# Gated linear attention by token, two heads at a time, in a two-layer encoder step

## What is computed

```python
    def step(S, inp):                       # one chunk, S is (64 x 128) a head
        qc, kc, vc, lac = inp
        cum = jnp.cumsum(lac, axis=1)
        last = cum[:, -1:]
        ref = 0.5 * last
        att = jnp.einsum('blhd,bshd->bhls', qc * jnp.exp(cum - ref), kc * jnp.exp(ref - cum))
        att = jnp.where(causal, att, 0.0)
        o = (jnp.einsum('bhls,bshe->blhe', att, vc)
             + jnp.einsum('blhd,bhde->blhe', qc * jnp.exp(cum), S))
        S = jnp.exp(last[:, 0])[..., None] * S + jnp.einsum('bshd,bshe->bhde', kc * jnp.exp(last - cum), vc)
        return S, o
...
    log_alpha = jax.nn.log_sigmoid(glr @ P['gla_w_gate'][j] + P['gla_b_gate'][j]) / GLA_TAU
    out_c = jax.nn.silu(gr) * _head_norm(o_c, P['gla_gn_g'][j])
```

## Times and profile before

| | |
|---|---|
| three runs | 1528.97, 1525.61, 1529.1 us, median 1528.97 |
| profiled execution | 1530.31 us, of which the span of its trace 1528.8 |
| busy | TensorE 1422.2 us, VectorE 714.6, ScalarE 494.3, GpSimd 85.0 |
| mean granted TensorE clock | 0.961 of full speed |
| items and decays of the GLA stage | about 773.9 to 947.2 us of the span |
| first mLSTM head | 947.2 to 967.7 us |

### The profile page before, as it was taken

One profiled execution on the slowest core, in us unless ns is written; L12 is line 12 of the kernel. 1 busy time (PEld: TensorE's weight loads), 2 busy tenths in 40 slices (PEclk: granted clock), 3 DMA queues, 4 the chain that ended last, 5 costly groups with the idle time before them and its releaser, 6 DMA issues.

```text
span 1528.8 us, 28545 instructions
## 1 busy us (share of the span) xinstructions
PE 1422.2 (93%) x11061; PEld 1346.7 (88%) x11061; DVE 714.6 (47%) x1243; ACT 494.3 (32%) x751; POOL 85.0 (6%) x101
## 2 busy tenths in 40 slices
PE   5999998989999999999879798998799999999997
PEld 3888887979999999999768686878799999999997
DVE  4664654564433333334663535774643333333344
ACT  4453354333222222222352324331332222222233
POOL 0000000001100110010000000000001001100100
PEclk9899999999999999999979798998899999999999
DMA  9444454665353335222212121331222232232222
GB/s 343 141 130 141 129 146 126 214 232 192 91 180 96 87 91 191 85 83 66 62 30 56 33 69 40 85 89 58 69 68 83 85 94 83 84 95 83 82 76 80
DMA packets 224520, 163.12 MB, mean 107 GB/s; under 512 B 9346, under 2 KB 209732, under 8 KB 224332
## 3 DMA queue, kind: packets, MB, share of 16 engines
q1 hardware_dynamic: 212864, 119.42, 26.8%
q10 hardware_dynamic: 6764, 25.30, 4.4%
q0 software_dynamic: 4832, 17.58, 3.6%
HBM read 158.68 MB, written 3.59 MB: 106 GB/s over the span
## 4 chain that ended last, share of the span: by engine, by line
PE 83%; DVE 6%; DMA 4%; ACT 3%; issue 3%; ACTq 1%; DVEq 0%; POOL 0%; POOLq 0%; SPq 0%
PE ring L555 71%; DMA mod_weight<-in_w_mod 2%; PE core_j L461 2%; DVE weight_low L423 1%; PE core_k L461 1%; DMA weight_raw<-in_a_w_out 1%; PE core_j L775 1%; ACT weight_high L418 1%; PE core_k L1159 1%; DMA mixer_area<-in_w_mod 1%; PE ring L1252 1%; PE core_k L1162 1%; ACTq L2050 1%; PE core_k L780 1%; DVE normed_low L653 0%
## 5 line engine op out<-in xcount | busy, mean ns | idle before, releaser
L555 PE MATMUL ring<-normed_high,weight_high 128*128 128x272 f32 x2128 | 453.6, 295 | 27.6 <-DVE normed_low L653 14.1
L555 PE MATMUL ring<-normed_high,weight_low 128*128 128x272 f32 x2128 | 446.3, 292 | 0.0
L555 PE MATMUL ring<-normed_low,weight_high 128*128 128x272 f32 x2128 | 445.9, 291 | 0.0
L555 PEld LDWEIGHTS ring<-normed_high,weight_high 128*128 128x128 f32 x2128 | 340.8, 192 | 36.9 <-issue 23.7
L555 PEld LDWEIGHTS ring<-normed_low,weight_high 128*128 128x128 f32 x2128 | 341.7, 193 | 0.0
L555 PEld LDWEIGHTS ring<-normed_high,weight_low 128*128 128x128 f32 x2128 | 339.0, 192 | 0.0
L423 DVE TENSOR_TENSOR weight_low<-weight_raw,weight_high 128x1024 fp32r<-128x1024 f32 x197 | 261.1, 1326 | 142.1 <-ACT weight_high L418 141.0
L418 ACT ACTIVATE weight_high<-weight_raw 128x1024 fp32r<-128x1024 f32 x197 | 207.0, 1051 | 180.0 <-PE ring L555 146.2
L555 PE MATMUL ring<-mixed_high,weight_high 128*128 128x272 f32 x960 | 203.9, 294 | 11.6 <-DVE weight_low L423 8.2
L555 PE MATMUL ring<-mixed_high,weight_low 128*128 128x272 f32 x960 | 201.5, 292 | 0.0
L555 PE MATMUL ring<-mixed_low,weight_high 128*128 128x272 f32 x960 | 200.9, 291 | 0.0
(11 more groups left out here) (370 smaller groups left out, 1026.0 us busy)
## 6 DMA issues: line engine op xcount, KB each, us to landing
weight_raw<-in_w_ffn_in SPq DMA_DIRECT2D x88, 512.0 KB, 4.0
mixer_area<-in_w_mod ACTq DMA_DIRECT2D x12, 2048.0 KB, 10.9
mod_weight<-in_w_mod POOLq DMA_DIRECT2D x16, 1024.0 KB, 5.9
weight_raw<-in_w_ffn_out SPq DMA_DIRECT2D x32, 512.0 KB, 4.1
weight_raw<-in_a_w_in SPq DMA_DIRECT2D x24, 512.0 KB, 5.7
weight_raw<-in_c_w_in SPq DMA_DIRECT2D x20, 512.0 KB, 4.2
mixer_area<-in_w_mod SPq DMA_DIRECT2D x7, 1024.0 KB, 13.6
weight_raw<-in_w_ffn_out SPq DMA_DIRECT2D x16, 384.0 KB, 3.4
```

Source lines behind the costliest of these rows:

```text
L555: last = pe.matmul(PS[p.slot][:, half, 0:HALF], w[n.slot][:, k, :], x[:, k, half * HALF:(half + 1) * HALF], start=(k == 0 and w is WH and ...
```

## The change

The GLA part is written anew.

- Decays: the two 16-row products write to `core_j` and `core_k`, between the two halves of the first item, and no longer through the ring. The gate rows of the mLSTM are turned later, before item 11.
- Scores: a head uses its own 64 rows of the key and query tiles as operands; the zeroed copies and their GpSimd memsets are gone.
- Key-value products: two products of 64 rows x 64 columns for each chunk, one a head, into the upper and lower half of one PSUM tile. One serial sum of states then serves both heads.
- Output: by token, the masked scores and queries as the stationary side, the values and states moving (128 columns).
- Norm: batch-norm statistics on ten blocks (five token blocks of two heads), one inverse root for both heads, the blocks normalised half by ScalarE and half by VectorE, then turned back by TensorE through the ring and multiplied by gain and gate.
- Order: items are value, key, query, value, gate, gate of pair 0, value, key, query, value of pair 1, u, gate, gate, o. SP's loads, waits and the tiles' places are changed to fit. In the first mLSTM head its q and k products stand ahead of its value product.

Cut to the parts that are spoken of:

```diff
+            for n, a in enumerate(GLA_COLS):
+                load_weight(sp, gla_w(n), CW, lambda: a)
+                if n == 1:
+                    sp.wait_ge(s_modp, FIRST_HALF + 12)
+                    gla_state(0)
+                if n == 8:
+                    sp.wait_ge(s_rexp, 2)
+                    for row, src in ((0, RA), (1, RI)):
+                        sp.dma_start(GATE_ROWS[row], src[0:HEADS, :]).then_inc(s_smw, 16)
+                if n == 9:
+                    gla_state(1)
+                if n == 10:
+                    ml_weights(0)
+                    sp.wait_ge(s_smw, 64)
+                    ml_decays(0)
+            sp.wait_ge(s_got, 2)
+            ml_states(0)
+            for h in range(1, HEADS):
+                load_weight(sp, ml_w(h, 0), CW, lambda: h * P + C_U)
+                load_weight(sp, ml_w(h, 1), CW, lambda: h * P + C_O)
+                ml_weights(h)
+                ml_decays(h)
+                ml_states(h)
             sp.wait_ge(s_rg, 1)
             sp.dma_start(out["m_p"][0].rearrange("a h -> h a"), RM[0:HEADS, TP - 1:TP],
...
+        def gla_kv_pe(pe, i):
+
+            pe.wait_ge(s_gvtok, 2 * i + 2)
+            pe.wait_ge(s_gatt, 2 * i + 2)
             for c in range(2 * NB):
                 r = slice(64 * (c % 2), 64 * (c % 2) + 64)
-                dst = (K, J)[c % 2][:, 0, (c // 2) * P:(c // 2 + 1) * P]
-                pe.matmul(dst, K4T[r, c // 2, :], VTG[r, c // 2, :], start=True, stop=True)
-            pe.matmul(K[:, 1, 0:P], K4T[0:TS, NB, :], VTG[0:TS, NB, :], start=True, stop=True).then_inc(s_gkv, 1)
-            fill()
-            pe.wait_ge(s_gst, n + 1)
+                for j in range(2):
+                    q = slice(64 * j, 64 * j + 64)
+                    pe.matmul((K, J)[c % 2][q, 0, (c // 2) * P:(c // 2 + 1) * P], K4T[r, c // 2, q],
+                              VTG[j][r, c // 2, :], start=True, stop=True)
+            for j in range(2):
+                q = slice(64 * j, 64 * j + 64)
+                mm = pe.matmul(K[q, 1, 0:P], K4T[0:TS, NB, q], VTG[j][0:TS, NB, :], start=True, stop=True)
...
+        def gla_out_pe(pe, i):
+
+            pe.wait_ge(s_gst, i + 1)
             pe.wait_ge(s_gs0, 16 * i + 16)
-            for c in range(2 * NB):
-                cols = slice(64 * c, 64 * c + 64)
-                pe.matmul(K[:, 0, cols], VTG[:, c // 2, :], AG[:, c // 2, 64 * (c % 2):64 * (c % 2) + 64],
-                          start=True, stop=(c == 0))
-                if c:
-                    pe.matmul(K[:, 0, cols], SG8[:, c - 1, :], Q3[j][:, cols], start=False, stop=True)
-            pe.matmul(K[:, 1, P:P + TS], VTG[0:TS, NB, :], AG[0:TS, NB, 0:TS], start=True, stop=False)
-            pe.matmul(K[:, 1, P:P + TS], SG0, Q3[j][:, TP:T], start=False, stop=True).then_inc(s_got, 1)
+            for j in range(2):
+                q = slice(64 * j, 64 * j + 64)
+                dst = (K, J)[j]
+                for b in range(NB):
+                    cols = slice(b * P, (b + 1) * P)
+                    if b:
+                        pe.matmul(dst[:, 0, cols], AG[j][:, b, :], VTG[j][:, b, :], start=True, stop=False)
+                    else:
+                        for r in (slice(0, 64), slice(64, P)):
+                            pe.matmul(dst[r, 0, cols], AG[j][:, b, r], VTG[j][:, b, :], start=True, stop=(r.start == 0))
+                    for c in (2 * b, 2 * b + 1):
+                        if c:
+                            pe.matmul(dst[64 * (c % 2):64 * (c % 2) + 64, 0, cols], Q3[q, 64 * c:64 * c + 64],
+                                      SG8[q, c - 1, :], start=False, stop=True)
+                pe.matmul(dst[0:TS, 1, 0:P], AG[j][0:TS, NB, 0:TS], VTG[j][0:TS, NB, :], start=True, stop=False)
+                mm = pe.matmul(dst[0:TS, 1, 0:P], Q3[q, TP:T], SG0[q], start=False, stop=True)
+            mm.then_inc(s_got, 1)
+
+        def gla_turn_pe(pe, i, j):
+
+            p = Turn(R_GLA + GLA_TURNED[i][j])
+            pe.wait_ge(*((s_on, i + 1) if j else (s_o, HEADS + i + 1)))
+            pe.wait_ge(s_free[p.slot], p.before)
+            for b in range(NB):
+                pe.transpose(PS[p.slot][:, 0, b * P:(b + 1) * P], ON2[:, j * (NB + 1) + b, :], IDENT)
+            pe.transpose(PS[p.slot][:, 1, 0:TS], ON2[0:TS, j * (NB + 1) + NB, :],
+                         IDENT[0:TS, 0:TS]).then_inc(s_otr, 1)
+
...
+            for n in (1, 2):
+                item(n)
+            gla_keys_pe(pe, 0)
+            gla_values_pe(pe, 0, 0)
+            item(3)
+            pe.wait_ge(s_k4tok, 1)
+            gla_scores_pe(pe, 0, 0)
+            pe.wait_ge(s_gvtok, 1)
+            gla_values_pe(pe, 0, 1)
+            item(4)
+            pe.wait_ge(s_gatt, 1)
+            gla_scores_pe(pe, 0, 1)
+            item(5)
+            gla_kv_pe(pe, 0)
+            item(6)
+            gla_out_pe(pe, 0)
+            for n in (7, 8):
+                item(n)
+            gla_keys_pe(pe, 1)
+            pe.wait_ge(s_on, 1)
+            gla_values_pe(pe, 1, 0)
+            item(9)
+            gla_turn_pe(pe, 0, 0)
+            pe.wait_ge(s_k4tok, 2)
+            gla_scores_pe(pe, 1, 0)
+            gla_turn_pe(pe, 0, 1)
+            pe.wait_ge(s_gvtok, 3)
+            gla_values_pe(pe, 1, 1)
+            item(10)
+            pe.wait_ge(s_gatt, 3)
+            gla_scores_pe(pe, 1, 1)
+            pe.wait_ge(s_gvtok, 4)
+            gate_rows_pe(pe)
+            item(11)
             pe.wait_ge(s_gtok, 1)
-            for i in range(2):
-                def item(j):
-                    project(pe, Turn(W_GLA, j, 6, i), Turn(R_GLA, j, 6, i))
-
-                def item_part(j, ks):
-                    project_part(pe, Turn(W_GLA, j, 6, i), Turn(R_GLA, j, 6, i), ks)
-
-                item(1)
-                if i == 0:
-                    pe.wait_ge(s_rexp, 2)
-                    for b in range(NB):
-                        pe.transpose(K[:, 0, 4 * b:4 * b + 4], RF[0:HEADS, b * P:(b + 1) * P], IDENT[0:HEADS, 0:HEADS])
...
+        def gla_moments_dve(dve, st, i):
+            dve.wait_ge(s_got, i + 1)
+            for j in range(2):
+                for b in range(NB + 1):
+                    n = P if b < NB else TS
+                    st.add(dve.bn_stats(BNG[0:n, j * (NB + 1) + b, :], gla_block(j, b)))
+
+        def gla_rstd_dve(dve, st, i):
+            st.wait()
+            for b in range(2 * NB + 2):
+                n = P if b % (NB + 1) < NB else TS
+                st.add(dve.bn_aggr(MVG[0:n, b, :], BNG[0:n, b, :]))
+            st.wait()
+            st.done(dve.tensor_scalar(VARG, MVG[:, :, 1], EPS, None, ALU.add))
+            rsqrt(dve, st, VARG, RSTDG, RTMPG)
+            dve.scalar_tensor_tensor(out=NMG, in0=MVG[:, :, 0], scalar=-1.0, in1=RSTDG, op0=ALU.mult,
+                                     op1=ALU.mult).then_inc(s_nv, 1)
+
+        def gla_normalise_dve(dve, st, i):
+            dve.wait_ge(s_otr, 2 * i)
+            for b in range(NB + 1):
+                n, c = P if b < NB else TS, NB + 1 + b
+                ins = dve.tensor_scalar(ON2[0:n, c, :], gla_block(1, b), MVG[0:n, c, 0:1], RSTDG[0:n, c:c + 1],
+                                        ALU.subtract, ALU.mult)
+                if b < NB:
+                    st.add(ins)
+            ins.then_inc(s_on, 1)
+
+        def gla_gated_dve(dve, st, i, j):
+            n = 2 * i + j
+            p = Turn(R_GLA + GLA_TURNED[i][j])
+            dve.wait_ge(s_otr, n + 1)
+            dve.wait_ge(s_gah, KD + DONE0 + n - 1 if i else KD + DONE0)
+            ring_done(dve, gla_r(GLA_G[i][j]))
+            gain = HGAIN[:, n + 4:n + 5]
+            st.add(dve.scalar_tensor_tensor(out=OBS[j][:, 0:TP], in0=PS[p.slot][:, 0, :], scalar=gain,
+                                            in1=SGATE[j][:, 0:TP], op0=ALU.mult, op1=ALU.mult))
+            dve.scalar_tensor_tensor(out=OBS[j][:, TP:T], in0=PS[p.slot][:, 1, 0:TS], scalar=gain,
+                                     in1=SGATE[j][:, TP:T], op0=ALU.mult, op1=ALU.mult).then_inc(s_free[p.slot], 1)
+            ring_done(dve, p)
+            dve.sem_inc(s_ob, 1)
+
+        def gla_low_dve(dve, n):
+
+            dve.wait_ge(s_gah, KD + DONE0 + n + 1)
+            dve.tensor_tensor(GL[:, n, :], OBS[n % 2], GH[:, n, :].bitcast(F32), ALU.subtract).then_inc(s_glo, 1)
```

Of VectorE's list for pair 1 and ScalarE's for the end of the stage:

```diff
+            gla_gate_dve(dve, 1, 1)
+            gla_moments_dve(dve, st, 1)
+            low(14)
+            gla_rstd_dve(dve, st, 1)
+            gla_normalise_dve(dve, st, 1)
...
+            high(14)
+            ml_weights_exp(act, st, 0)
+            normalise(1)
+            ml_gate(act, 0)
```

762 lines of the change are left out of this document (392 added, 370 removed).

## The result

The changed kernel takes 1480.8 us, the median of four runs (1477.09 to 1481.41), against 1528.5 in four runs of the kernel before: ratio 0.9687, 95% interval 0.9665 to 0.9708. The forecast was 1481. The profiled execution is the fastest of the four, 1477.1 us with a span of 1475.4; what follows is read from it.

The account below looks back on a forecast made before the run. TensorE was taken to set the time, losing 23.9 us idle and to a lower clock. 1530.3 - 49.4 (stretch A) + 1.7 (stretch B) = 1482.6; the runs' median lies 1.3 lower, so 1481 us; range 1470 to 1500.

Parts of the forecast that it names:

- stretch A: From 773.9 to the last GLA output product: 113 us, no TensorE idle time, clock 1.00; gain 49.4 us.
- stretch B: From the last output product to the end of the first mLSTM head: new load wait, 33.3 against 31.6 us, loss 1.7.
- output: Output products by token in the GLA stage: 4.1 us a head, bounds 2.4 and 5.5; four heads 16.4.
- One sign of being wrong: On TensorE's timeline: steps over .3 us between a 64-row product and a 128-row one would show the forecast wrong.
- The key-value term: A pair's 32 key-value products with the small ones, going two by two: 2.3 us a pair, 4.6 in all.
- The lower bound, 1.3: A pair's key-value products if four run at once: 1.3 us, making the time 2 us less.
- The change of shape: Output products switching between 128 and 64 array rows: about .1 us a change, ten changes a head, 1.0.
- The rival that wanted 1.6: Array shape changes in stretch A, 30 more than before, cost 1.6 us each or more: kernel slower, 1532 at 1.7; chance .04.
- The idle time: TensorE ahead of the first mLSTM head's k product, behind SP's weight load: idle 8.8 us.
- VectorE as the bound: Rival: VectorE's serial work sets the time in stretch A, three places each 4 us late, 1497 us; chance .14.
- the three places: In a GLA pair, states, root and the low part after it: VectorE margins of 1.3 to 2.2 us.
- The clock at its old level: Rival: TensorE's clock stays at 0.87 through stretch A, 17 us more, 1498 us; chance .08.

Follow-up runs that it names:

- e2: Changed kernel with each head's output products grouped by shape, three changes of array shape in place of ten; 1475.9 us, ratio 0.9649.
- e1: Changed kernel with the next mLSTM head's two weights loaded ahead of SP's wait for the last GLA output product; 1471.9 us, ratio 0.9623.
- b2: Kernel before without the GLA norm's mean and variance products on TensorE and its waits for them; 1517.1 us against 1527.2, ratio 0.9927.
- e5: Changed kernel with one wait put in: item 7 waits until the norm of pair 0 is done; 1489.0 us, ratio 0.9763.
- e8: e3 with ScalarE's tanh of the mLSTM gate ahead of its half of the normalising; 1464.4 us, ratio 0.9587.
- b1: Kernel before with only the decay products moved, to core_j and core_k between the first item's halves; 1528.75 us against 1527.2, ratio 1.0015.
- b3: b1 plus mLSTM gate rows turned behind item 2, its weight split earlier, SP's waits later; 1531.0 us against 1528.0 for the kernel before, ratio 1.0022.
- e7: Changed kernel with the ten statistics of pair 0 taken three more times on VectorE; 1485.1 us, ratio 0.9721.
- e3: Changed kernel with the changes of e1 and e2 together; 1468.5 us, ratio 0.9604.

## Why the prediction was right

The forecast was 1481, the median 1480.8. The mechanism came out as forecast: no wait in stretch A, the clock near 1.00, one new wait in stretch B behind SP's load. That the number is right to 1 us is luck: errors of 1 to 4 us in several terms cancelled.

- **Stretch A, 112.8 forecast, 111.0 measured.** That TensorE would not wait and would run at 1.00 held but for the fall at the end (.99). Terms by the timeline: key-value products 2.3 forecast, 1.4 a pair with the small ones; output 4.1 forecast, 3.74 a head; together 3.2 too much. The scores took 1.26 and not 1.4, the decays 2.0 and not 1.8, a turned result .7 and not .54. The fall cost 1.2. One sign of being wrong is there by its letter, steps of .42 and .37 between products of 128 and 64 rows where over .3 was named; but .22 and the forecast's own .1 are already .32, and the head came out under its term.
- **The key-value term** was sized by the twins of the earlier trace rows, two at once. Its 2.3 is also less than these rows give: 16 twins at the 1.09 us of eight are 2.2, with .42 for the small ones 2.6. Four ran at once, and it took 1.4. The lower bound, 1.3, and the sentence on the Trainium skill's page TensorEngine Tiling (Array Packing), section Tiling Modes, had it; the changed kernel's trace agrees with that sentence (1.4 measured), and rows of before could not show it.
- **The change of shape**, .1 from the earlier trace rows, is .12 to .15 by e2. The .1 compared a product of 32 moving columns with one of 128, so it may have been read low. The rival that wanted 1.6 is out by ten times: at .15 the 58 changes that it counts cost 9 us in all.
- **Stretch B, 33.3 forecast, 32.75 measured**, with two errors that hid each other. The k product started 14.2 behind the output and not 16.0, for the weight landed 4.9 us after its issue and not 6.0, and the rest was .7 shorter. Behind the k product 18.5 passed and not 17.3: at the higher level it is 16.7 (e1) and not 16.0, and the clock cost 1.9 and not 1.3. The idle time was 5.0 and not 8.8: 1.8 less by the earlier k product, and 2.0 less since item 13 ran at the lower level, 8.1 us for 6.1. That the new wait was SP's load is shown by e1.
- **Where the gain came from.** At the higher level TensorE's work in stretch A before was, as an estimate, some 119 us (13 items 79.4, the rest by the prices of the earlier trace rows and the mean and variance). So of 51.2 us, 8 are products that went, 23.9 idle time, and the other 19 the clock. b2, which drops the norm's products and its waits, gains 10 to 12, of the same order as the 8. That a wait costs clock behind it is measured at e5 (2.4 us for one wait of 8.2) and e8 (1.7 for 1.8). The kernel before had eighteen waits in this stretch, 23.9 us, and six times at the lower level (in windows of 2 us, from 776, 794, 804, 854, 906 and 930), each of them begun at or right behind a wait. Their sum, 19, is the estimate's and no single run's.
- **The sum of parts.** The prediction added up the end state and did not ask what each part brings alone, rightly: b1 and b3 bring nothing, b2 10, the whole 48. The early waits were ends of one chain through VectorE, GpSimd and ScalarE. The changed kernel cuts it (16.3 us and not 28.8 to the keys); which of its parts does, the values as the first item, the memsets that went or the order of the lists, no run tells. Pairing the heads was not tried by itself either.
- **Rivals.** VectorE as the bound: not so. TensorE waits nowhere in stretch A, and at one of the three places the slack is 2.7 us (e7); the slack of the others was not measured. The clock at its old level: it was at .99. Slower through shapes: no.

## What to carry to other kernels

When an engine waits at many places, find the step that all the waits end on before moving instructions: moving TensorE's early work forward gained nothing while one PSUM place was freed by a late chain. Then price the whole new order as if nothing waited, and check the slack of each chain on the other engines; that sum was good to 2 us here, with terms that were out by as much and more. A load behind a semaphore that it doesn't need is worth a look each time: it cost 7 us here. Products of one array shape should stand together. And where two kernels ran on different chips or in different executions, compare a stage between two instructions that both have: it showed 3.4 us between e3 and e8, which the times could not.

## What was unexpected of the hardware

- The clock of TensorE can fall from the higher to the lower level while it is busy: in each of six profiles with outputs that change shape at nearly every product, for 3 to 10 us, in none of four with the same products grouped by shape. One profile of each kernel was read, and the cause is open.
- A change of the array's shape between products costs .12 to .15 us at the higher clock level (e2).
- 32 instructions of 64 x 64 products for two heads take as long as 16 of 64 x 128 for one: four started every .11 us.
- Fourteen instructions of 64 x 64 state products, alternating between the upper and lower half of the result, took 1.01 us, .07 each, against .12 for a full product's.
